# A streaming encoder step: the query projection as a set of seven block products

## The chip, the cores and the metric

The kernel runs on one core of a Trainium2 chip. The metric is the device time of one execution in microseconds. Before the change it was 788.36 us, the median of 3 runs (787.86 to 789.13).

## The reference, cut to what matters

The reference is one layer of an encoder for 528 frames of a new stream (16 meta frames and 512 of the prompt) and 64 frames of a running one, with caches of 1024 keys and values.

```
hp = layer_norm(concat(meta, x_prompt), ln_in_g, ln_in_b)      # 528 x 1024
hs = layer_norm(x_sample, ln_in_g, ln_in_b)                    #  64 x 1024
z = h @ w_in + b_in
u, q, k, v, ga, gb = split(z, ...)        # u, q, k, v: 512 columns each; ga, gb: 1024 each
pooled  = trailing window means of u, minus u
attn    = stick_breaking_attention(q, k and v with the cache), 8 heads of 64
mix = sigmoid(ga) * (pool_out @ w_br_pool) + sigmoid(gb) * (attn @ w_br_attn)
h = layer_norm(ALPHA * h + mix @ w_out + b_out, ...)
h = layer_norm(ALPHA * h + square(relu(h @ w_mlp1 + b1)) @ w_mlp2 + b2, ...)
```

The queries `q` of the 512 prompt frames and the 64 sample frames (576 columns; the meta frames have no queries), scaled by 1/8, are the part that the change computes in another way.

## The kernel before, in words

Everything lies transposed: channels on the 128 partitions, frames along the row. Every product is computed in fp32r in three matmuls, high part by high part, high by low and low by high, so each weight and each operand is rounded into a high part by ScalarE (ACT) and the rest is subtracted into a low part by VectorE (DVE). Weights come as units of 128 x 1024: all eight chunks of the input for 128 output channels. SyncE (SP) loads them into four raw slots; `split` makes `whi` and `wlo` in two slots. A unit is 48 matmuls: 2 halves of the frames, 8 chunks, 3 parts.

*The first normalisation* works on `r0`, 8 chunks of channels by 592 frames in two halves of 296. For the second half VectorE scales a chunk (`scale0`, L2258), ScalarE adds the bias and rounds it to `h_hi` (L1481), and VectorE makes `h_lo` (L2264), chunk 0 to chunk 7. The counter `n0_scaled` is 16 when the last chunk is scaled.

*The keys* (`keys_pair`, L877 to L880) are four units. Units 0 and 1 run together for a half of the frames, in the two banks of `lin`, the second some chunks behind the first; then units 2 and 3. The second half of units 0 and 1 follows the normalisation chunk by chunk. `key_out(m, h)` on ScalarE (L1494) moves the bank to `k_t` and frees it: `key_out(0, 1)` frees the bank of unit 2's second half and `key_out(1, 1)` that of unit 3's.

*The queries* are four more units (`linear`, L757 to L759) from the 576 frames in two halves of 288; ScalarE and VectorE move them to `q_t` and `q_s` (by head, for the sample frames). Then come `scores(0)` (L978), the first scores of the sample frames against the cache, and the value units (L938 to L940). Before its first matmul `scores(0)` waits for the keys' cache, for the masks of GpSimd (POOL), and for `consts`, a counter that ScalarE raises behind the copies of two small triangular matrices, `tri_r` (L1541) and `below_r` (L1542). `weighted_values(0)` is the first to want the values' cache.

*Sets.* Most of the MLP runs in twelve sets of seven block products after the scheme of Strassen and Winograd: the weights of four output units and the operand are cut in two by two blocks, seven products of sums of blocks take the place of eight. The seven weight operands (`W_AL` to `W_GA`) come from five loaded blocks, two of them with a second block added by an accumulating load that GpSimd issues, and from two additions on VectorE (`x_sum`, `dp_sum`); `op_hi` (L1859) and `op_lo` (L2717) split them. `block_product` (L1274 to L1276) issues the 24 matmuls of one product (2 output banks, 4 chunks, 3 parts). A product waits for its low part (`s_lo`), its moving operand and its banks; ScalarE copies two results (`first_copy`, `second_copy`) and VectorE adds two (`third_sum`, `fourth_sum`). The moving sums (`hs_sum`: V5, V6, T3, V4, each of four chunks by 288 frames) are made once for all sets (L2812, L2816, L1928).

The order of each engine's work is the order of its program, written out by hand; engines meet only at counting semaphores.

## Time and profile before

| | us |
|---|---|
| median of 3 runs | 788.36 |
| lowest, highest | 787.86, 789.13 |
| the profiled execution's own time | 788.11 |
| its span, first to last instruction | 786.4 |
| TensorE busy | 773.2 (98%) |
| VectorE busy | 521.4 (66%) |
| ScalarE busy | 427.4 (54%) |
| GpSimd busy | 145.7 (19%) |
| granted clock, mean | 0.995 |

The profile is of one execution, and its terms are counted against its own 788.11 us. PE stands for TensorE's matmuls and PEld for its weight loads, which lie beside them. Matmuls are pipelined: a record of some 0.3 us starts every 0.13 us, so the pitch is read from the starts and not from the durations.

### The profile page before, as it was taken

How to read it: one execution, taken by the hardware profiler on the slowest of the kernel's cores; microseconds unless marked ns; L12 is line 12 of the kernel's file. 1: busy time of each engine (PE TensorE's matmuls, PEld its weight loads, DVE VectorE, ACT ScalarE, POOL GpSimd, SP SyncE). 2: the span in 40 equal slices, each digit the busy share in tenths (PEclk: the TensorE clock that was granted, in tenths of full speed). 3: DMA queues.
4: the chain of work that ended last, by engine and by line, in shares of the span. 5: the costliest groups of instructions: out<-in, count | busy, mean ns of one | idle time of the engine just before them, and what ended most of it. 6: DMA issues, size and time to landing. Idle time of an engine off the chain costs nothing.

```text
span 786.4 us, 14056 instructions
## 1 busy us (share of the span) xinstructions
PE 773.2 (98%) x5720; PEld 746.3 (95%) x5720; DVE 521.4 (66%) x762; ACT 427.4 (54%) x666; POOL 145.7 (19%) x195
## 2 busy tenths in 40 slices
PE   8999999999999999999999999999999999999995
PEld 6999889999989899999999999999999999999994
DVE  5833334756546466887769897778876897665744
ACT  4632445656556465564446566488436773477324
POOL 2100000390321110005560000000000000000456
PEclk9999999999999999999999999999999999999998
DMA  8732231111120212225111556655767566633203
GB/s 293 289 119 81 80 117 54 54 55 59 54 81 30 79 37 72 82 93 176 55 55 30 132 159 163 180 131 173 188 161 188 150 165 168 162 106 135 81 2 120
DMA packets 27070, 90.57 MB, mean 115 GB/s; under 512 B 2864, under 2 KB 7104, under 8 KB 26624
## 3 DMA queue, kind: packets, MB, share of 16 engines
q1 hardware_dynamic: 22592, 74.26, 27.5%
q0 software_dynamic: 4000, 15.10, 10.7%
q8 instruction: 45, 0.74, 0.4%
q10 hardware_dynamic: 416, 0.33, 0.1%
q14 instruction: 17, 0.14, 0.1%
HBM read 84.84 MB, written 4.85 MB: 114 GB/s over the span
## 4 chain that ended last, share of the span: by engine, by line
PE 93%; DVE 2%; ACT 2%; issue 1%; DMA 1%; SPq 0%; DVEq 0%; ACTq 0%
PE lin L757 9%; PE z L1274 8%; PE z L1275 8%; PE z L1276 8%; PE lin L758 8%; PE lin L759 8%; PE z L1013 3%; PE lin L1274 3%; PE lin L1275 3%; PE lin L1276 3%; PE lin L1151 3%; PE lin L1152 3%; PE lin L1153 3%; PE lin L1290 2%; PE lin L1289 2%; PE lin L1288 2%
## 5 line engine op out<-in xcount | busy, mean ns | idle before, releaser
L757 PE MATMUL lin<-h_hi,whi 128*128 128x288 f32 (+1 forms) x448 | 133.8, 299 | 0.0
L758 PE MATMUL lin<-h_lo,whi 128*128 128x288 f32 (+1 forms) x448 | 132.5, 296 | 0.0
L759 PE MATMUL lin<-h_hi,wlo 128*128 128x288 f32 (+1 forms) x448 | 132.0, 295 | 0.0
L757 PEld LDWEIGHTS lin<-h_hi,whi 128*128 128x128 f32 x448 | 84.2, 188 | 1.3 <-issue 1.1
L758 PEld LDWEIGHTS lin<-h_lo,whi 128*128 128x128 f32 x448 | 84.2, 188 | 0.1
L759 PEld LDWEIGHTS lin<-h_hi,wlo 128*128 128x128 f32 x448 | 84.3, 188 | 0.0
L2717 DVE TENSOR_TENSOR wlo<-raw,whi 128x1024 fp32r<-128x1024 f32 x48 | 58.7, 1224 | 20.8 <-ACT whi L1859 20.8
L1859 ACT ACTIVATE whi<-raw 128x1024 fp32r<-128x1024 f32 x48 | 50.7, 1056 | 37.1 <-PE z L1276 24.5
L2120 DVE TENSOR_TENSOR wlo<-raw,whi 128x1024 fp32r<-128x1024 f32 x41 | 50.9, 1241 | 28.6 <-ACT whi L1381 26.6
L1381 ACT ACTIVATE whi<-raw 128x1024 fp32r<-128x1024 f32 x38 | 40.0, 1053 | 50.6 <-PE lin L759 32.6
L1274 PE MATMUL z<-f_ops,whi 128*128 128x288 f32 x176 | 52.2, 296 | 0.2
L1275 PE MATMUL z<-f_ops,whi 128*128 128x288 f32 x176 | 51.6, 293 | 0.0
L1276 PE MATMUL z<-f_ops,wlo 128*128 128x288 f32 x176 | 51.4, 292 | 0.0
L3236 POOL DMA_DIRECT2D raw<-w_sets x12 | 10.4, 870 | 152.6 <-DMA raw<-w_sets 152.6
L2717 DVE TENSOR_TENSOR third_lo<-raw,third_hi 128x1024 fp32r<-128x1024 f32 x24 | 29.4, 1223 | 11.7 <-ACT third_hi L1859 11.5
L1859 ACT ACTIVATE third_hi<-raw 128x1024 fp32r<-128x1024 f32 x24 | 25.3, 1056 | 21.4 <-PE z L1276 10.1
L2341 DVE SCALAR_TENSOR_TENSOR sa<-z,sa 128x512 f32<-128x512 f32 (+4 forms) x25 | 19.8, 795 | 25.6 <-ACT sa L1564 25.4
L1274 PEld LDWEIGHTS z<-f_ops,whi 128*128 128x128 f32 x176 | 33.0, 188 | 0.6 <-issue 0.6
L1276 PEld LDWEIGHTS z<-f_ops,wlo 128*128 128x128 f32 x176 | 33.1, 188 | 0.0
L1275 PEld LDWEIGHTS z<-f_ops,whi 128*128 128x128 f32 x176 | 33.0, 188 | 0.0
L2304 DVE TENSOR_SCALAR gates<-lin,vecs 128x288 f32<-128x288 f32 x16 | 8.2, 515 | 34.7 <-PE lin L759 34.7
L3238 POOL DMA_DIRECT2D raw<-w_sets x12 | 10.4, 863 | 106.7 <-DMA raw<-w_sets 106.7
(456 smaller groups left out, 2590.7 us busy)
## 6 DMA issues: line engine op xcount, KB each, us to landing
raw<-w_stream SPq DMA_DIRECT2D x64, 512.0 KB, 3.3
raw<-w_sets SPq DMA_DIRECT2D x48, 512.0 KB, 3.9
raw<-w_sets POOLq DMA_DIRECT2D x24, 512.0 KB, 5.6
w_fifth<-w_sets SPq DMA_DIRECT2D x12, 512.0 KB, 7.0
r<-x_t SPq DMA_DIRECT2D x8, 296.0 KB, 5.1
kcache<-k_cache SPq DMA_DIRECT2D x1, 2048.0 KB, 10.2
vcache<-v_cache SPq DMA_DIRECT2D x1, 2048.0 KB, 8.9
y<-r SPq DMA_DIRECT2D x8, 160.0 KB, 1.8
```

The costliest lines, as they stand in the source:

```text
L757: pe.matmul(out, w_h, hi, start=first, stop=False)
L758: pe.matmul(out, w_h, lo, start=False, stop=False)
L759: return pe.matmul(out, w_l, hi, start=False, stop=last)
L1013: last = pe.matmul(zf[:, d:d + w], stationary[:, :], part[:, src + at:src + at + w], start=False, stop=True, skip_group_check=True)
L1151: pe.matmul(out, w_h, hi, start=first, stop=False)
L1274: pe.matmul(out, w_h, hi, start=s < 2 and i == 0, stop=False, skip_group_check=True)
L1275: pe.matmul(out, w_h, lo, start=False, stop=False, skip_group_check=True)
L1276: last = pe.matmul(out, w_l, hi, start=False, stop=i == PRS - 1, skip_group_check=True)
L1381: nc.scalar.activation(whi[:, j % SPLIT, :], raw[:, j, :], ACT.Copy).then_inc(hi_split, 1)
L1859: nc.scalar.activation(op_home(o)[0], set_home(source_slot(s)), ACT.Copy).then_inc(s_hi, 1)
L2120: tt(wlo[:, j % SPLIT, :], raw[:, j, :], whi[:, j % SPLIT, :].bitcast(F32), ALU.subtract)\
L2717: tt(home[1], set_home(source_slot(s)), home[0].bitcast(F32), ALU.subtract).then_inc(s_lo, 1)
```

## The change

The four query units go from the stream of weights and become one more set, the first of thirteen (`FIRST = 1` is the first of the old ones; the counters get offsets). Its output blocks go through `query_block` to `q_t` and `q_s`. Its moving sums come from `r0`: V5, V6 and V4 on VectorE, T3 with one subtraction and four small instructions on GpSimd, and `xs_round` and `xs_low` split them. Its first and every third weight operand, its fifth block and two results have rooms of their own in the memory of the values' cache and the normalisation, so the values' cache is loaded behind the whole set, as are the pool's state and the units behind them. Three of the eight warm matmuls at the start write to another bank.

```diff
 # constants
-SETS = [("out", 0, 0), ("out", 0, 1)]
+SETS = [("query", 0, 0), ("out", 0, 0), ("out", 0, 1)]
+FIRST = 1
...
 # SyncE, behind the loads of units 0 to 3
-            load_unit(1, 0)
-            load_unit(1, 1)
+            for n, slot, block, landed in ((1, c, 2, si_base), (2, a, 0, al_in), (3, d, 2, ap_base), (4, b, 1, de_in),
+                                           (4, g, 3, ga_in)):
+                sp.wait_ge(lo_split, n)
+                load_block(0, slot, block, landed)
             sp.dma_start(bv[:, :], bv_d).then_inc(bv_in, 16)
             sp.dma_start(kcache[:, :, :], kc_d).then_inc(kc_in, 16)
-            load_unit(1, 2)
-            load_unit(1, 3)
+            sp.wait_ge(s_lo, W_SI + 1)
+            sp.wait_ge(x_made, 1)
+            load_unit(1, 0, first=True)
...
+            sp.wait_ge(s_lo, W_GA + 1)
+            sp.wait_ge(op_done, OPS)
             sp.dma_start(vcache[:, :, :], vc_d).then_inc(vc_in, 16)
             sp.dma_start(wpool[:, :, :], wpool_d).then_inc(wpool_in, 16)
...
 # TensorE, behind the keys
-            for m in range(4):
-                linear(1, m, N_Q + m, h_hi, h_lo, META, HA)
...
+            for s in range(OPS):
+                block_product(0, s)
...
 # ScalarE
             for k in range(4, KC):
                 norm0_hi(k, 1)
+            op_hi(0)
             key_out(0, 1)
-            act.wait_ge(unit_in[0], 32)
-            act.wait_ge(unit_done, 1)
-            nc.scalar.activation(whi[:, 0, :], raw[:, 0, :], ACT.Copy).then_inc(hi_split, 1)
-            for m in range(1, 4):
-                key_out(m, 1)
+            xs_round(V5)
+            op_hi(1)
+            key_out(1, 1)
+            key_out(2, 1)
+            xs_round(V6)
+            key_out(3, 1)
 
             act.wait_ge(bq8_done, 1)
-            for m in range(4):
-                split_next(1, m)
-                act.wait_ge(half_done, N_Q + m + 1)
-                nc.scalar.activation(q_t[:, m, 0:HA], lin[:, 0, 0:HA], ACT.Identity, bias=bq8[:, m:m + 1],
-                                     scale=SB_SCALE).then_inc(bank_free[0], 1)
+            act.wait_ge(q_zero, 1)
+            for s in range(OPS):
+                if s == 1:
+                    first_copy(0)
+                    xs_round(T3)
+                elif s == 2:
+                    second_copy(0)
+                elif s == 3:
+                    xs_round(V4)
+                elif s == 6:
+                    query_block(C12)
+                if s + 2 < OPS:
+                    op_hi(s + 2)
+                if s in (4, 5):
+                    query_block(C11 if s == 4 else C22)
+                if s == 5:
+                    act.wait_ge(op_done, 5)
+                    split(1, 0)
+            act.wait_ge(op_done, 6)
+            split(1, 1)
+            query_block(C21)
 
             act.wait_ge(made, 7)
             nc.scalar.activation(tri_r[:, :], tri[:, :], ACT.Copy)
...
 # VectorE, behind the low part of chunk 7 and a product of 4 columns
+            xs_sum(V5)
+            op_lo(0)
+            x_sum(0)
+            xs_sum(V6)
+            xs_low(V5)
+            op_lo(1)
+            xs_sum(V4)
+            xs_low(V6)
+            for s in range(OPS):
+                if s == 3:
+                    third_query()
+                elif s == 5:
+                    fourth_query()
+                if s + 2 < OPS:
+                    op_lo(s + 2)
+                if s == 1:
+                    dp_sum(0)
+                    xs_low(T3)
+                elif s == 3:
+                    xs_low(V4)
             split(1, 0)
...
 # GpSimd, in the middle of the masks
+            add_blocks(0)
...
+            pool.wait_ge(vecs_in, 16)
+            nc.gpsimd.tensor_tensor(xb_diff[:, :], vecs[:, V_LNIN_B + PRS:V_LNIN_B + KC],
+                                    vecs[:, V_LNIN_B:V_LNIN_B + PRS], ALU.subtract).then_inc(made, 1)
             pool.wait_ge(n0_scaled, 2 * KC)
-            pool.dma_start(u_t[:, :, UP:UP + STATE], state_d).then_inc(state_in, 16)
+            c = slice(META + HA, T)
+            nc.gpsimd.tensor_tensor(xs_sums[:, T3 - V5, :, :], r0[:, PRS:KC, c], r0[:, 0:PRS, c], ALU.subtract)\
+                .then_inc(made, 1)
+            pool.wait_ge(made, 13)
+            for k in range(PRS):
+                x_k = xs_sums[:, T3 - V5, k, :]
+                nc.gpsimd.tensor_scalar(x_k, x_k, 1.0, xb_diff[:, k:k + 1], ALU.mult, ALU.add).then_inc(made, 1)
```

## Rows read from the trace of the kernel before

**Rows 1.** The page: TensorE's busy time; the granted clock in 40 slices.
```profile
PE 773.2 (98%) x5720; PEld 746.3 (95%) x5720; DVE 521.4 (66%) x762; ACT 427.4 (54%) x666; POOL 145.7 (19%) x195
PEclk9999999999999999999999999999999999999998
```
**Rows 2.** Waits of PE: us in total, times, longest.
```profile
PE lin L877 <- ACT h_hi L1481: 0.8, 1, 0.8
```
**Rows 3.** Timeline of PE (start us, us): first query matmul, first behind the queries.
```profile
49.63 0.30 PE L757 MATMUL lin<-h_hi,whi 128*128 128x288 f32 x1
...
75.12 0.38 PE L978 MATMUL z<-q_s,k_t 128*128 128x128 f32 x2
```
**Rows 4.** Lines of the block products (ns min/median/max, first and last start).
```profile
L1274 PE MATMUL z<-f_ops,third_hi x80: 291/294/371, 454.6 to 677.1; 128*128 128x288 f32 x80
...
L1276 PE MATMUL z<-hs_hi,wlo x96: 293/295/298, 506.0 to 722.0; 128*128 128x288 f32 x96
```
**Rows 5.** Timeline of VectorE, at the end of the normalisation.
```profile
40.21 0.52 DVE L2264 SCALAR_TENSOR_TENSOR h_lo<-r,vecs,h_hi 128x296 fp32r<-128x296 f32 x1
40.91 0.53 DVE L2264 SCALAR_TENSOR_TENSOR h_lo<-r,vecs,h_hi 128x296 fp32r<-128x296 f32 x1 [0.17 <-ACT h_hi L1481]
41.35 0.20 DVE L2300 TENSOR_SCALAR bq<-vecs 128x4 f32<-128x4 f32 x1
```
**Rows 6.** GpSimd's groups by form (busy us, mean ns, idle before).
```profile
L3105 POOL TENSOR_SCALAR win<-win 128x591 f32<-128x591 f32 x4 | 3.5, 876 | 0.4
...
L3243 POOL TENSOR_TENSOR sum<-r 128x576 f32<-128x576 f32 x1 | 1.4, 1430 | 47.5 <-DVE r L2934 47.5
```
**Rows 7.** Timelines of GpSimd and VectorE, where they meet.
```profile
391.73 0.80 POOL L3211 TENSOR_TENSOR sumsq<-sumsq,sq 128x288 f32<-128x288 f32 x1
...
391.81 1.03 DVE L2571 SCALAR_TENSOR_TENSOR h_lo<-r,vecs,h_hi 128x288 fp32r<-128x288 f32 x1
...
158.27 1.80 POOL L3111 TENSOR_TENSOR u_t<-win,u_t 128x591 f32<-128x591 f32 x1
...
159.34 1.81 DVE L2120 TENSOR_TENSOR wlo<-raw,whi 128x1024 fp32r<-128x1024 f32 x1 [0.15 <-ACT whi L1381]
```
**Rows 8.** Timeline of PE in the keys: last of unit 0, first of unit 3.
```profile
41.71 0.30 PE L880 MATMUL lin<-h_lo,whi 128*128 128x296 f32 x1
...
45.12 0.29 PE L877 MATMUL lin<-h_hi,k_hi 128*128 128x296 f32 x1
```
**Rows 9.** Lines of the sets' sums, roundings and splits (ns min/median/max).
```profile
L2812 DVE TENSOR_TENSOR hs_sums<-r x1: 1351/1351/1351, 437.1 to 437.1; 128x1152 f32<-128x1152 f32 x1
...
L1928 ACT ACTIVATE hs_hi<-hs_sums x4: 1146/1150/1157, 478.6 to 491.1; 128x1152 fp32r<-128x1152 f32 x4
...
L2816 DVE SCALAR_TENSOR_TENSOR hs_sums<-hs_sums,vecs,r x4: 512/512/514, 460.8 to 462.1; 128x288 f32<-128x288 f32 x4
...
L2717 DVE TENSOR_TENSOR wlo<-raw,whi x48: 1217/1224/1228, 453.1 to 710.7; 128x1024 fp32r<-128x1024 f32 x48
...
L1859 ACT ACTIVATE whi<-raw x48: 1042/1060/1064, 449.8 to 709.7; 128x1024 fp32r<-128x1024 f32 x48
```
**Rows 10.** Timeline of ScalarE at the end of the queries.
```profile
72.14 0.50 ACT L1537 ACTIVATE q_t<-lin,bq 128x288 f32<-128x288 f32 x1 [2.07 <-PE lin L759]
...
72.74 0.30 ACT L1542 ACTIVATE below_r<-below 128x128 fp32r<-128x128 f32 x1
```
**Rows 11.** Loads: the page's issues (us to landing); timelines of SP and GpSimd.
```profile
raw<-w_sets POOLq DMA_DIRECT2D x24, 512.0 KB, 5.6
...
14.11 2.78 SPq L663 DMA_DIRECT2D raw<-w_stream  x2
...
40.61 0.97 POOL L3079 DMA_DIRECT2D u_t<-pool_state  x1 [5.55 <-DVE r L2258]
```
**Rows 12.** Timeline of PE at its end; a window (busy, PEclk, DMA, GB/s).
```profile
776.15 0.61 PE L1338 MATMUL z<-sq,inv 128*128 128x256 f32 x2
...
779.00:779.50 0.50, 0.00 (x0) 0.00 (x0) 0.47 (x2) 0.06 (x1) 0.50 (x2) 0.53 0.00 0
```

More of the change, by code:

```diff
@@ L847, in _ @@
             pe.wait_ge(made, 1)
-            for _ in range(WARM):
-                warm()
+            for n in range(WARM):
+                if n < 3:
+                    pe.matmul(z[:, 2, bass.ts(n, P)], inv_d[:, :], inv_d[:, :], start=n == 0, stop=True,
+                              skip_group_check=True)
+                else:
+                    warm()
             for p in range(KC // 2):
@@ new lines, in block_product @@
+            def block_product(t, s):
+                kind, p, g = SETS[t]
+                o, f = OPS * t + s, MOVING[ORDER[s]]
+                home, (chain, copy, second, third) = op_home(o), bank_pairs(t)
+                pair = (chain, second, chain, copy, chain, second if kind == "out" else third, chain)[s]
+                pe.wait_ge(s_lo, o + 1)
+                banks_ready(t, s)
+                moving_ready(t, s)
+                for j in range(2):
+                    out = one_bank(pair, j)
+                    if t < FIRST and s == 0:
+                        pe.wait_ge(bank_free[j], N_K + 4)
+                    for i in range(PRS):
+                        if t == FIRST and j == 0 and i in (0, PRS - 1):
+                            ready = max(F_AT[f, n] for n in (range(PRS - 1) if i == 0 else (i,)))
+                            pe.wait_ge(f_lo_done, ready + 1)
+                        at = slice((2 * i + j) * P, (2 * i + j + 1) * P)
+                        w_h, w_l = home[0][:, at], home[1][:, at]
+                        hi, lo = (f_op(f, i, 0), f_op(f, i, 1)) if kind == "out" else hs_op(f, i, t)
+                        pe.matmul(out, w_h, hi, start=s < 2 and i == 0, stop=False, skip_group_check=True)
+                        pe.matmul(out, w_h, lo, start=False, stop=False, skip_group_check=True)
+                        last = pe.matmul(out, w_l, hi, start=False, stop=i == PRS - 1, skip_group_check=True)
+                last.then_inc(op_done, 1)
@@ L1279, in _ @@
-            for t in range(N_SETS):
+            for t in range(FIRST, N_SETS):
                 for s in range(OPS):
@@ new lines, in query_block @@
+            def query_block(c):
+                chain, copy, _, third = bank_pairs(0)
+                if c == C22:
+                    act.wait_ge(z_summed, 2)
+                else:
+                    act.wait_ge(op_done, {C11: 4, C12: 6, C21: 7}[c])
+                scale = -SB_SCALE if c in (C22, C21) else SB_SCALE
+                for j in range(2):
+                    m = 2 * j + int(c in (C22, C21))
+                    src = q_fourth[:, j, :] if c == C22 else one_bank({C11: copy, C12: third, C21: chain}[c], j)
+                    if c in (C11, C21):
+                        last = nc.scalar.activation(q_t[:, m, 0:HA], src, ACT.Identity, bias=bq8[:, m:m + 1], scale=scale)
+                    else:
+                        nc.scalar.activation(q_t[:, m, HA:SEQ], src[:, 0:SEQ - HA], ACT.Identity, bias=bq8[:, m:m + 1],
+                                             scale=scale)
+                        for e in range(2):
+                            rows = slice(64 * e, 64 * e + 64)
+                            last = nc.scalar.activation(q_s[rows, 2 * m + e, :], src[rows, SEQ - HA:HA], ACT.Identity,
+                                                        bias=bq8[rows, m:m + 1], scale=scale)
+                    last.then_inc(relu_done, 1)
@@ new lines, in xs_sum @@
+            def xs_sum(o):
+                x = xs_sums[:, o - V5, :, :]
+                first, second = slice(META, META + HA), slice(META + HA, T)
+                if o == V5:
+                    tt(x, r0[:, 0:PRS, first], r0[:, 0:PRS, second], ALU.subtract).then_inc(hs_made, 1)
+                elif o == V4:
+                    dve.wait_ge(hs_made, 1 + PRS)
+                    for k in range(PRS):
+                        stt(out=x[:, k, :], in0=xs_sums[:, V6 - V5, k, :], scalar=vec(V_LNIN_B + PRS + k),
+                            in1=r0[:, PRS + k, first], op0=ALU.subtract, op1=ALU.subtract).then_inc(hs_made, 1)
+                else:
+                    dve.wait_ge(hs_made, 1)
+                    for k in range(PRS):
+                        stt(out=x[:, k, :], in0=xs_sums[:, 0, k, :], scalar=vec(V_LNIN_B + PRS + k),
+                            in1=r0[:, PRS + k, second], op0=ALU.add, op1=ALU.add).then_inc(hs_made, 1)
```

356 lines of the change are left out of this document (194 added, 162 removed).

## Prediction

> **What bounds the kernel now.** I read the page first: TensorE (PE) is busy in 773.2 of 786.4 us, and its granted clock is full in every slice but the last [rows 1]. Then the waits of PE: behind the first microseconds the longest in the whole span is one of 0.8 us [rows 2], for the first normed frame; the others are smaller still. So what PE issues, one matmul after the other, is the time, and an edit is worth what it takes from PE's list or adds to its waits. The stage of the change is the queries. Its first matmul starts at 49.63 us and the first of the stage behind it at 75.12 [rows 3]: 25.49 us for 192 matmuls, 132.8 ns each. The block products that the kernel has already run at the same pitch: from 454.6 to 722.0 us it issues 2016 matmuls [rows 4], 132.7 ns each, with no wait of weight in all twelve sets.
>
> **Fewer matmuls.** Four units of 48 are 192. One set has seven products of 2 x 4 x 3, which are 168. The 24 that go are worth 24 x 132.8 ns = 3.19 us. This is all that the change can bring.
>
> **What must be ready for the set, and where it is put.** Every step that follows goes by the three other engines in the last 10 us of the keys, where the new work is queued.
>
> *The third moving sum on GpSimd.* It waits for all 16 normed frames. The last scaling is the instruction in front of the low part at 40.21 us in VectorE's list (its `n0_scaled` comes near 40.3) [rows 5]. The sum is a subtraction of 1152 elements with both inputs in SBUF. GpSimd's 576-element one takes 1430 ns and its 288-element ones 0.80 us [rows 6, 7]: 2.2 ns an element and 0.16 us, so 2.7 us here. The trace shows what such an instruction does to a VectorE one with two SBUF inputs that starts beside it. At 391.81 us a 288-element low part takes 1.03 us in place of 0.52 (as at 40.21), with a GpSimd addition running from 391.73 to 392.53; at 159.34 a 1024-element one takes 1.81 in place of 1.22, with one running to 160.07 [rows 5, 7]. In both VectorE ends as if it had begun 0.1 to 0.2 us before GpSimd's record ended (392.84 - 0.52 = 392.32; 161.15 - 1.22 = 159.93): it waits for the whole GpSimd instruction. In the new kernel VectorE holds the way until 40.73 (the low part of chunk 6), then is idle till 40.91, as it waits for ScalarE [rows 5]. GpSimd starts there, at about 40.6, and ends at 43.3. The low part of chunk 7, at 40.91 now, is then done at about 43.6 in place of 41.44. It is the operand of PE's matmul at 41.71 [rows 8]. PE waits until 43.65: **1.95 us**, with everything behind it. From both sides: nothing, if VectorE's instruction gets in first or both share the way; 2.2 us, if GpSimd's is not held up at its start. I take the value of the two rows, which agree.
>
> The Trainium skill, page "SBUF — State Buffer", section "SBUF: two separate sides", states this as a lock: the pair of ports that VectorE and GpSimd share is held for the whole instruction by the one that starts first, and counts for a VectorE instruction with two SBUF inputs against a GpSimd one that reads SBUF. By that rule this term is about 2 us, and the trace agrees with its 1.03 and 1.81 us; were the ports a shared bandwidth instead, the term would be under 0.7 us.
>
> *The first rounding ahead of the second key output.* `xs_round(V5)` and `op_hi(1)` stand in ScalarE's list ahead of `key_out(1, 1)`, which frees the bank that PE wants for the first matmul of unit 3 at 45.12 [rows 8]. `xs_round` needs the sum V5 of VectorE: 1.35 us [rows 9], behind the low part and the tiny product at 41.35 [rows 5]. With the 1.95 us above: low part until 43.6, tiny product, then the wait for one of GpSimd's four small sums (591 elements take 0.88 us in the mean [rows 6], so some 0.5 us each) until 43.9, the sum until 45.2, the rounding (1.15 [rows 9]) until 46.4, `op_hi(1)` (1.06 [rows 9]) until 47.35, `key_out` (as long as the output at 72.14, 0.50 [rows 10]) until 47.8. PE wants the bank at 45.12 + 1.95 = 47.07. **0.76 us** of wait. Without the GpSimd term the same sum reads 42.83, 44.0, 45.0, 45.4 against 45.12: 0.4 us with the restart. With two small GpSimd sums in the way it is 1.2. The keys end 2.7 us late, at 52.34.
>
> *The set.* Product s starts at 52.34 + 3.19 s. VectorE's list up to the low part of the third operand is the first sum, two sums of four pieces (4 x 0.43 each), two low parts of 1.35, three low parts of weights and one sum of weights (1.22 each) [rows 9], 12.4 us at full durations and 11.4 back to back. With some 0.4 us for each of GpSimd's small sums it is done at 56.7, and product 2 wants it at 58.7: hidden, with 2.0 us to spare. From there each weight operand is released by a product two steps back, as in the sets of before, and the copies, the third and fourth sum (0.8 us) fit between; the tightest is the third sum, with about 1.1 us to spare. The blocks come long before: SP issues the first at 14.1 us where it issues unit 4 now, the accumulating load takes 5.6 us to land, and it is wanted at 46 [rows 11]. The two loads that GpSimd issues wait for blocks in its list, ahead of the masks; these are wanted by PE at 75 us, and GpSimd is idle for the 5.6 us before 40.61 [rows 11]. The values' cache is issued behind product 6, and SP's loads of units behind it; the cache is wanted behind the scores and all four value units, the next unit of weights (raw slot 0, the first of the pooling branch) behind three of them. Each costs nothing; if one of these covers were gone its lateness counts in full.
>
> *From the set to the scores.* This is the wait that the text of the diff hides. `scores(0)` waits for `consts`, which ScalarE raises behind two small copies, and these stand behind `query_block(C21)`, which waits for the **last** product. Now they end at 73.04 (the second is at 72.74), behind the output of the half that PE finished 3.2 us before its end [rows 3, 10]. After the change: 0.20 us from PE's end to ScalarE, two outputs at a pitch of 0.40 and the first copy at 0.20 (together the 0.60 from 72.14 to 72.74), 0.30 for the second, and 0.05 to PE: 0.2 + 0.8 + 0.2 + 0.3 + 0.05 = **1.55 us** in which PE has nothing. At its lower end 1.3 (a quicker release), at its upper one 2.0 (`split(1, 1)`, put ahead of it, ends 0.6 us before and may be late). The warm matmuls that change their bank, and the counters that are renumbered, cost nothing: the count is the same.
>
> **The sum.** Against the profiled execution's own 788.11 us: 788.11 - 3.19 + 1.95 + 0.76 + 1.55 = 789.18. Behind the scores PE alone sets the order, so the shift is kept to the end. That execution lies 0.25 us below the median of 788.36, so I forecast **789.4**. A difference of 0.2% (1.6 us) is about what a measurement of this kernel can tell from none.
>
> **The rivals.**
> *A: the GpSimd sum does not stop the low part.* The sum is then 788.11 - 3.19 + 0.4 + 1.55 = 786.9, on the median's scale 787.1. For it: GpSimd's start after its release isn't shown for this place (its load at 40.61 now starts 0.3 us after the release [rows 11]), and many pairs in the trace run side by side with no loss. Against it: both rows of a pair with two SBUF inputs.
> *B: the waits are hidden and the whole 3.2 us is seen*, 785.2. It wants both the bank and `consts` early; the list of ScalarE speaks against it.
> *C, slower: VectorE falls behind and product 2 waits.* Its list of 11.4 us and GpSimd's small sums have 2.0 us to spare in front of product 2. If each of those sums (0.9 us each at worst) stops it in full, or the four-piece sums are stopped by each other, it is 2 us later yet; from the point where 2.0 us are used up each further us is one of PE. With 1.5 us over: 790.9. A late accumulated block would have the same face.
> *D, slower: the clock.* PE's last matmuls start at 776.15, and the granted clock, still 1.00 at 779.0, falls towards 0.50 (1.2 GHz; 0.53 in the mean to 779.5) [rows 12], over 2 us after they end. The longest wait that I forecast is 1.95 us, just short of that; the one of 0.8 us left the clock at full [rows 1, 2]. If it falls, every us at the lower level costs half: with 2 to 4 us of it 790.4 to 791.4.
>
> **How the numbers follow.** Forecast 0.58, its own range 788.7 to 790.4; A 0.17; B 0.06; C 0.13; D 0.06. The range from 786.6 to 791.4 takes in A and most of C and D and leaves out B and the far ends of C. Faster by over 0.2% (below 786.8): B, a third of A, and a little of the rest, 0.15. Slower by over 0.2% (above 789.9): C, D and a fifth of the forecast, 0.30. Within: 0.55.
>
> **What would show it.** In the profile after: the low part of chunk 7 (`h_lo`) as long as 2.7 us at 40.9, with GpSimd's 1152-element subtraction beside it, and PE idle before its `h_lo` matmul at 43.6; PE idle again for about 0.8 us before a key matmul near 47, released by ScalarE's `k_t`; 168 matmuls of the set in 22.3 us; and PE idle for about 1.5 us before the first matmul with `q_s`, released by `below_r`. If the low part takes 0.53 us, A is right. If PE waits inside the set for VectorE, C is. If PE's granted clock has a dip near 43 us, D is. The forecast is wrong if the first matmul with `q_s` comes before 75.6 us or behind 76.9.

## The result and the profile after

The changed kernel takes **792.41 us** (median of 5 runs, 791.38 to 793.42) where the kernel before takes 787.86 beside it: ratio 1.0055, interval 1.0044 to 1.0066. In a second comparison (`a1_after`) it was 791.66 against 788.01, ratio 1.0046, 1.0032 to 1.0061. So it is slower by 3.6 to 4.3 us by the ratios. Forecast were 789.4 and at most 791.4. Wherever this document says how much an edit brings, it compares ratios to the kernel before, taken beside each run, and 0.001 is 0.79 us; the interval of a ratio is some 1 us to either side. Two executions of the runs below were slow ones and are left out of every figure: 2673.15 us in `a1_after` (with it that run's median would be 792.11, a number that some of the expectations use) and 838.29 us in `e2_bank_first`, which is the profiled one, so that its profile is not read.

The profiled execution of the changed kernel takes 791.38 us, with a span of 789.6. Its page begins:

```profile
PE 771.1 (98%) x5695; PEld 743.8 (94%) x5696; DVE 537.7 (68%) x770; ACT 440.2 (56%) x687; POOL 156.1 (20%) x203
...
PEclk9999999999999999999999999999999999999998
```

TensorE has 2.1 us less to do [rows 1] and the span is 3.2 us longer, so it waits more. The waits of PE in the whole span (us in total, times, longest):

```profile
PE z L1079 <- ACT below_r L1672: 2.3, 1, 2.3
PE lin L922 <- DVE h_lo L2364: 1.9, 2, 1.7
PE z L897 <- DVE pair L2309: 1.2, 2, 0.6
...
PE lin L919 <- issue: 0.5, 1, 0.5
```

The first, the second and the last of these are new beside [rows 2]. The one between them (`pair`) stands at the head of the kernel, in a part that the change leaves as it was: VectorE adds pieces of x in pairs, each as soon as its load has landed. VectorE starts the fourth of these sums between 6.8 and 8.5 us in the profiles of this case, in the kernel before at 7.32, here at 8.14; this is called the head below. The timeline of PE around the new waits (start us, us; in brackets the idle time before and its releaser):

```profile
42.45 0.29 PE L920 MATMUL lin<-h_hi,wlo 128*128 128x296 f32 x1
44.49 0.40 PE L922 MATMUL lin<-h_lo,whi 128*128 128x296 f32 x1 [1.75 <-DVE h_lo L2364]
...
47.85 0.30 PE L922 MATMUL lin<-h_lo,k_hi 128*128 128x296 f32 x1
48.66 0.37 PE L919 MATMUL lin<-h_hi,k_hi 128*128 128x296 f32 x1 [0.51 <-issue]
...
53.24 0.29 PE L1017 MATMUL lin<-h_hi,q_third_hi 128*128 128x288 f32 x1
...
75.40 0.30 PE L1019 MATMUL lin<-xs_hi,q_third_lo 128*128 128x288 f32 x1
77.98 0.46 PE L1079 MATMUL z<-q_s,k_t 128*128 128x128 f32 x2 [2.28 <-ACT below_r L1672]
```

The set runs from 53.24 to 75.53 (the last start and one pitch of 0.13): 22.29 us for 168 matmuls, and none of them waits. What released the wait for the low part stands in the timeline of VectorE,

```profile
41.77 2.66 DVE L2364 SCALAR_TENSOR_TENSOR h_lo<-r,vecs,h_hi 128x296 fp32r<-128x296 f32 x1 [0.17 <-ACT h_hi L1533]
```

and in that of GpSimd beside it:

```profile
41.24 2.87 POOL L3241 TENSOR_TENSOR xs_sums<-r 128x1152 f32<-128x1152 f32 x1 [5.18 <-DVE r L2358]
44.22 5.35 POOL L3246 TENSOR_SCALAR xs_sums<-xs_sums,xb_diff 128x288 f32<-128x288 f32 x4
```

The low part takes 2.66 us where it took 0.53 [rows 5]; GpSimd's record of the subtraction ends at 44.11, and VectorE's low part ends at 44.43 as if it had begun at 43.9. What released the two others, the bank and the constants, stands in the timeline of ScalarE:

```profile
48.07 0.49 ACT L1546 ACTIVATE k_t<-lin,vecs 128x296 f32<-128x296 f32 x1
...
74.68 0.62 ACT L1605 ACTIVATE q_s<-z,bq 64x64 f32<-64x64 f32 x2
75.32 1.06 ACT L1433 ACTIVATE whi<-raw 128x1024 fp32r<-128x1024 f32 x1
76.41 0.89 ACT L1599 ACTIVATE q_t<-lin,bq 128x288 f32<-128x288 f32 x2
77.19 0.31 ACT L1671 ACTIVATE tri_r<-tri 128x128 fp32r<-128x128 f32 x1
77.39 0.31 ACT L1672 ACTIVATE below_r<-below 128x128 fp32r<-128x128 f32 x1
```

The output that frees the bank ends at 48.56, PE starts at 48.66. The first matmul with `q_s` starts 2.86 us later than before [rows 3]. By starts of PE, this is the account: head +0.82, low part +1.96 (1.75 of idle time and the restart), bank +0.67 (48.66, where 47.99 would follow at the pitch), set -3.20 (22.29 for 25.49), constants +2.45 (77.98 against 75.53), and 0.16 in small pieces. The head varies from execution to execution with the landing. Without it, the profile says that the change costs some **1.9 us**. The ratios say 3.6 to 4.3. So two things are to be found: what each wait is made of, and where about 2 us more come from that this profile doesn't have.

### The profile page after: what moved, and what is told of

Same layout as the page of the kernel before. It is cut to its first block, busy times and chain, and to the rows that moved or that the text cites. A ratio compares the mean times of both kernels' runs of the same rounds, so it can differ in the third digit from the quotient of the medians.

```text
span 789.6 us, 14042 instructions
## 1 busy us (share of the span) xinstructions
PE 771.1 (98%) x5695; PEld 743.8 (94%) x5696; DVE 537.7 (68%) x770; ACT 440.2 (56%) x687; POOL 156.1 (20%) x203
## 4 chain that ended last, share of the span: by engine, by line
PE 90%; ACT 3%; DVE 3%; issue 2%; DMA 1%; SPq 0%; DVEq 0%; ACTq 0%
PE z L1017 9%; PE z L1018 9%; PE z L1019 9%; PE lin L794 7%; PE lin L795 7%; PE lin L796 7%; PE lin L1017 3%; PE lin L1018 3%; PE lin L1019 3%; PE z L1114 3%; PE lin L1252 3%; PE lin L1253 3%; PE lin L1254 3%; PE lin L1342 2%; PE lin L1340 2%; PE lin L1341 2%
## 5 line engine op out<-in xcount | busy, mean ns | idle before, releaser
L794 PE MATMUL lin<-h_hi,whi 128*128 128x288 f32 (+1 forms) x384 | 114.9, 299 | 0.0
L795 PE MATMUL lin<-h_lo,whi 128*128 128x288 f32 (+1 forms) x384 | 113.6, 296 | 0.0
L796 PE MATMUL lin<-h_hi,wlo 128*128 128x288 f32 (+1 forms) x384 | 113.2, 295 | 0.0
L794 PEld LDWEIGHTS lin<-h_hi,whi 128*128 128x128 f32 x384 | 72.2, 188 | 1.3 <-issue 1.1
L795 PEld LDWEIGHTS lin<-h_lo,whi 128*128 128x128 f32 x384 | 72.2, 188 | 0.1
L796 PEld LDWEIGHTS lin<-h_hi,wlo 128*128 128x128 f32 x384 | 72.3, 188 | 0.0
L3209 POOL DMA_DIRECT2D raw<-w_sets x13 | 11.5, 882 | 153.3 <-DMA raw<-w_sets 153.3
L3211 POOL DMA_DIRECT2D raw<-w_sets x13 | 11.3, 866 | 116.3 <-DMA raw<-w_sets 116.3
```

What stands on the lines that cost most here:

```text
L794: pe.matmul(out, w_h, hi, start=first, stop=False)
L795: pe.matmul(out, w_h, lo, start=False, stop=False)
L796: return pe.matmul(out, w_l, hi, start=False, stop=last)
```

## The experiments

Theory at the start: three waits (GpSimd's subtraction, the bank, the constants), each to be had back by one move in a list. Rivals: the low part is late because the query units have moved, not because of GpSimd; VectorE's list is too long; and the granted clock of TensorE, which shows no dip in this profile.

**Each wait by itself.** `e1_sum_behind`, GpSimd waits for VectorE's first sum and so for the low part in front of it:

```diff
             pool.wait_ge(n0_scaled, 2 * KC)
+            pool.wait_ge(hs_made, 1)
             c = slice(META + HA, T)
```

> The changed kernel with one edit: GpSimd's subtraction of 1152 elements waits for VectorE's first moving sum as well. Theory of the shared way: the low part of chunk 7 takes 0.53 us in place of 2.66, TensorE's wait of 1.75 us for it is gone, 1.7 to 2.0 us less in all. If the low part were late for another reason (ScalarE's rounding, the frames), nothing changes. The wait for the bank of unit 3 may stay at 0.3 to 0.7 us.

Measured: 788.96, ratio 1.0013 (1.0004 to 1.0022), 1.0 us above the kernel before. The wait for the low part is gone, and only one new long one is left:

```profile
PE z L1079 <- ACT below_r L1672: 2.2, 1, 2.2
...
PE lin L1017 <- DVE wlo L2429: 0.3, 1, 0.3
```

This one edit brings 2.6 to 3.3 us. By the starts of its profile it should bring 1.5: the low part's 1.96 are gone and the bank's wait falls from 0.67 to 0.28, but 0.4 and 0.6 us come at two places in the set (product 0's second bank, and operand 2). So over a microsecond more comes back than was waited.

`e3_copies_first`, the copies of the constants ahead of ScalarE's part of the set:

```diff
             act.wait_ge(q_zero, 1)
+            act.wait_ge(made, 7)
+            nc.scalar.activation(tri_r[:, :], tri[:, :], ACT.Copy)
+            nc.scalar.activation(below_r[:, :], below[:, :], ACT.Copy).then_inc(consts, 1)
             for s in range(OPS):
...
             query_block(C21)
 
-            act.wait_ge(made, 7)
-            nc.scalar.activation(tri_r[:, :], tri[:, :], ACT.Copy)
-            nc.scalar.activation(below_r[:, :], below[:, :], ACT.Copy).then_inc(consts, 1)
```

> The changed kernel with one edit: the copies tri_r and below_r, which raise consts, ahead of the set and not behind its last output. Theory of the waits: TensorE's 2.3 us before the first matmul with q_s falls to 0.2 us or less, 2.1 to 2.5 us less in all. Rival: the scores then wait for the third output block (ScalarE ends it at 75.3 us, the set ends at 75.5) and half of the gain stays away. Theory of the clock: with this longest wait gone the executions that lie 1 to 2 us above the profiled one come down more than it does.

Measured: 788.54, ratio 1.0003 (0.9994 to 1.0012). PE has no wait at the scores; the one for the low part stays (2.0, of which 1.75 at 44.82). The edit brings 3.4 to 4.1 us, again more than its wait of 2.45 (and its own profile has half clock behind the low part, see below).

`e2_bank_first`, the output that frees unit 3's bank ahead of the rounding:

```diff
             key_out(0, 1)
+            key_out(1, 1)
             xs_round(V5)
             op_hi(1)
-            key_out(1, 1)
```

> The changed kernel with one edit: key_out(1, 1) ahead of xs_round(V5) and op_hi(1). Theory of the waits: the wait of 0.5 to 0.7 us before unit 3 is gone and nothing else moves, 0.6 us less. Rival: the bank was free anyway and the 0.5 us of issue is something else; no change.

Measured: 792.21, ratio 1.0052 (1.0039 to 1.0066), nothing that stands out from the changed kernel's 1.0055 and 1.0046. It was run once more, as `a2_bank_first`, to see where its 0.67 us go.

> The changed kernel with the output of unit 1's second bank ahead of the rounding and the high part, once more, since its gain was 0.1 to 0.2 us where 0.6 were expected. If the wait moves on, the profile shows no wait at the first matmul of unit 3 and 0.4 us or more at the second bank of product 0, released by the last key output, which stands behind V6's rounding. If it is the clock, unit 3 stands in a stretch at half clock in which the bank would have been free in time anyway, and the edit is worth nothing there.

Measured: 791.68, ratio 1.0039 (1.0025 to 1.0053). In its profile the wait of 0.5 is gone and nothing has taken its place between 43.3 and 75 us: the bank was the wait, and the first branch (it moves on) is wrong. The second is borne out by the profiles in which half clock comes behind the low part (below): the kernels `e3_copies_first` and `e7_split_last` have the changed kernel's order, and PE doesn't wait for the bank in them. In them ScalarE frees the bank at 48.88 and 48.58, and PE, at half clock, comes to it only after that. So the profiles say that the edit is worth 0.67 in some executions and nothing in others; by the medians its gain can't be told from nothing.

`e4_all_three`, the three edits together:

> The changed kernel with its three waits of TensorE taken away: GpSimd's third moving sum also waits for VectorE's first one (so it starts behind the low part of chunk 7), key_out(1, 1) stands ahead of xs_round(V5) and op_hi(1), and the two copies that raise consts stand ahead of the set. Theory of the waits: the profile loses 1.96 + 0.66 + 2.45 = 5.1 us against the changed kernel's 791.4, so some 786.3 us, about 1.6 us under the kernel before; the first matmul with q_s starts near 73 us. Theory of the set (the set itself, its loads or what follows costs the time): over 790 us. Theory of the clock (in the executions beside the profiled one the granted clock falls in the waits of 2 us): the spread of the changed kernel, 791.4 to 793.4, shrinks to under 1 us, and no execution has a mean clock under 0.995.

Measured: **786.41**, ratio 0.9977 (0.9968 to 0.9986): faster than the kernel before, by 1.8 us (1.6 were forecast) and not by 3.2. All of its mean clocks are 0.995 to 0.997. Two waits that the three had covered are left in it; PE's waits:

```profile
PE lin L1017 <- ACT k_t L1546: 0.5, 1, 0.5
PE lin L1017 <- DVE wlo L2429: 0.3, 1, 0.3
```

What makes them stands in the timeline of VectorE,

```profile
43.74 3.72 DVE L2415 TENSOR_TENSOR raw<-raw 128x1024 f32<-128x1024 f32 x1
47.38 2.78 DVE L2445 SCALAR_TENSOR_TENSOR xs_sums<-xs_sums,vecs,r 128x288 f32<-128x288 f32 x4
```

and in that of GpSimd:

```profile
42.83 3.55 POOL L3242 TENSOR_TENSOR xs_sums<-r 128x1152 f32<-128x1152 f32 x1 [7.72 <-DVE xs_sums L2436]
46.49 3.38 POOL L3247 TENSOR_SCALAR xs_sums<-xs_sums,xb_diff 128x288 f32<-128x288 f32 x4
```

The subtraction no longer stops the low part; it stops the sum of the blocks, the third large operation behind the low part (3.72 us for 1.22), and the four small operations stop V6's sum (2.78 for 1.80). The last key output stands behind V6's rounding, so the second bank of product 0 is late, and operand 2's low part too.

**GpSimd alone.** `m1_before_sum` adds only the subtraction to the kernel before (and lets the copies of the constants wait for the higher count that goes with it, which makes no wait of PE at the scores in its profile):

```diff
...
-            act.wait_ge(made, 7)
+            act.wait_ge(made, 12)
             nc.scalar.activation(tri_r[:, :], tri[:, :], ACT.Copy)
...
             pool.wait_ge(n0_scaled, 2 * KC)
+            c = slice(META + HA, T)
+            nc.gpsimd.tensor_tensor(spare[:, :, :], r0[:, PRS:KC, c], r0[:, 0:PRS, c], ALU.subtract).then_inc(made, 1)
```

> The kernel before with one thing added: GpSimd subtracts 1152 elements a lane of the normed frames from 1152 others, into room that nobody reads, as soon as the last piece is scaled. The rest, the four query units as units among it, stands as before. If the subtraction stops VectorE's low part of chunk 7 for its whole length, that part takes about 2.7 us where it took 0.5, the first matmul that reads it waits about 1.8 to 1.9 us, and the time is 1.8 to 2 us above the kernel before. If only the move of the query units made the wait, the low part keeps its 0.5 us and the time stays within 0.3. If a wait of 2 us at this place also lowers TensorE's granted clock in most executions, the time is 2.7 to 3.2 us above the kernel before, and the mean granted clocks of the executions lie at 0.992 to 0.994 where those of the kernel before lie at 0.995 to 0.997.

Measured: 791.10 against 788.01, ratio 1.0037 (1.0024 to 1.0050), 2.9 us; mean clocks 0.994 to 0.995. The timeline of VectorE:

```profile
41.20 2.66 DVE L2265 SCALAR_TENSOR_TENSOR h_lo<-r,vecs,h_hi 128x296 fp32r<-128x296 f32 x1 [0.18 <-ACT h_hi L1482]
```

That of PE:

```profile
43.92 0.52 PE L881 MATMUL lin<-h_lo,whi 128*128 128x296 f32 x1 [1.75 <-DVE h_lo L2265]
44.24 0.45 PE L878 MATMUL lin<-h_hi,whi 128*128 128x296 f32 x1
44.48 0.45 PE L879 MATMUL lin<-h_hi,wlo 128*128 128x296 f32 x1
...
47.20 0.42 PE L878 MATMUL lin<-h_hi,k_hi 128*128 128x296 f32 x1
47.44 0.32 PE L879 MATMUL lin<-h_hi,k_lo 128*128 128x296 f32 x1
47.60 0.30 PE L881 MATMUL lin<-h_lo,k_hi 128*128 128x296 f32 x1
```

The subtraction makes the whole wait, with no other part of the change in the kernel: that the moved query units make it is out. And here is what the first profile of the changed kernel didn't have. Behind the wait the matmuls go at a pitch of 0.25 us and not 0.136, and the windows of this profile (busy time of PE, PEld, DVE, ACT, POOL; granted clock, DMA share, GB/s) say why:

```profile
43.00:44.00 1.00, 0.08 (x1) 0.08 (x1) 0.94 (x2) 0.00 (x0) 1.00 (x2) 1.00 0.00 0
44.00:45.00 1.00, 1.00 (x5) 1.00 (x6) 0.00 (x0) 0.52 (x2) 0.46 (x1) 0.52 0.00 0
45.00:46.00 1.00, 1.00 (x6) 1.00 (x6) 0.04 (x1) 0.93 (x1) 0.00 (x0) 0.50 0.22 31
46.00:47.00 1.00, 1.00 (x6) 1.00 (x6) 1.00 (x1) 0.30 (x1) 0.00 (x0) 0.50 0.00 0
47.00:48.00 1.00, 1.00 (x7) 1.00 (x7) 0.19 (x1) 0.21 (x1) 0.00 (x0) 0.77 0.00 0
```

TensorE is granted the lower of its two levels, 1.2 GHz for 2.4, from just behind 44.0 to about 47.5 us, while it is busy again. 13 matmuls at 0.11 us more each are 1.4 us.

**The changed kernel again.** `a1_after`, no edit:

> The changed kernel as it is, on the chip of the runs beside it. The waits of its first profile should come back: 1.9 us for the low part of chunk 7, 0.8 for a bank of unit 3, 2.3 for the copied constants. If the microsecond by which its median lies above its profiled execution comes from TensorE's clock, executions with a mean granted clock of 0.992 to 0.994 take about 1 us more than those with 0.996, and a profile of such an execution shows a stretch below 1.00 behind one of the waits that the first profile has at full clock. If it comes from the loads' landing, the first chunks start later in it and the clocks are alike.

Measured: 791.66. The waits come back (2.2 for `below_r`, 2.0 for `h_lo`, 0.5 for the bank), and its profiled execution has a mean clock of 0.994; the windows of PE:

```profile
44.00:48.00 4.00, 3.51 (x26) 3.29 (x25) 4.00 (x5) 2.74 (x4) 4.00 (x3) 1.00 0.00 0
...
77.00:78.00 1.00, 1.00 (x6) 1.00 (x6) 0.00 (x0) 0.00 (x0) 0.00 (x0) 0.50 1.04 442
78.00:79.00 1.00, 1.00 (x7) 1.00 (x6) 0.00 (x0) 0.00 (x0) 0.00 (x0) 0.50 1.03 442
79.00:80.00 1.00, 1.00 (x7) 1.00 (x6) 0.00 (x0) 0.00 (x0) 0.00 (x0) 0.50 1.05 420
```

This time the fall comes behind the wait for the constants (PE starts again at 76.72) and not behind the low part. Over ten executions of the changed kernel: two with a mean clock of 0.996 at 790.0 and 791.4; four with 0.994 at 791.7 to 793.1; four with 0.992 at 792.3 to 793.4. Each step of 0.002 is one stretch of 3.4 us at half clock (3.4 x 0.5 / 790 = 0.002). The mean alone is a blunt sign, though: behind the last matmuls of every profile the clock stands at half for another 5 to 8 us, as in [rows 12], and that alone makes it 0.995 to 0.997. So 0.995 can hide one stretch (`e3_copies_first`, profiled with one) or none (`e6_round_later`); 0.994 and 0.992 go with one and two in the profiles.

**The constants' wait.** `e7_split_last` was to test that ScalarE's list makes it:

```diff
-            split(1, 1)
             query_block(C21)
+            split(1, 1)
             act.wait_ge(made, 7)
```

> The changed kernel with one edit: ScalarE's second split of the values' weights (1.06 us) goes behind the last query block's two outputs, so the outputs and the copies of the constants begin at the end of the set and not 0.85 us later. If the wait before the first matmul with q_s is ScalarE's queue (split, outputs, copies), it falls from 2.3 us to 1.2 to 1.5, and the time by 0.8 to 1.1. If that wait is set by something that doesn't stand in this queue, it stays at 2.3. What could take the gain back: the values' first product needs the split, and would then wait at its start by up to 0.3 us.

Measured: 792.73, ratio 1.0059 (1.0047 to 1.0071), and a wait of 2.6, not 1.2 to 1.5. (One of its six executions, 794.70, has a mean clock of 0.945; without it the median is 792.24.) A miss, and the edit's own fault: the split stands behind the outputs, but still ahead of the copies, and these are what raises `consts`. The list adds up to it all the same: outputs 0.10 us behind PE's end at 76.53, 0.78 for them, 0.94 for the split, 0.50 for the two copies, 0.26 to PE at 79.11. In its profile both waits are followed by half clock (0.50 from 45 to 48 and from 80 to 82 us), at a mean of 0.992.

`e8_split_behind` puts the split behind the copies too.

> The changed kernel with ScalarE's second split of the values' weights behind the last query block's outputs and behind the copies of the constants too, so that from the set's end only outputs (0.89) and copies (0.5) stand ahead of the first matmul with q_s. If the 2.3 us there are ScalarE's list and nothing else, the wait falls to 1.3 to 1.6. The time then falls by 0.8 to 1.0 where the clock stands as it did, and by 1.5 to 2.3 (to 790 to 791) if the shorter wait also leaves the clock at full speed behind it, which the mean clocks would show (0.994 and above where the changed kernel has 0.992 to 0.994). If the wait is set by something else it stays at 2.3.

Measured: 790.64, ratio 1.0029 (1.0018 to 1.0040), 1.3 to 2.1 us under the changed kernel. The timeline of ScalarE:

```profile
74.56 0.89 ACT L1599 ACTIVATE q_t<-lin,bq 128x288 f32<-128x288 f32 x2 [0.53 <-PE lin L1019]
75.34 0.31 ACT L1670 ACTIVATE tri_r<-tri 128x128 fp32r<-128x128 f32 x1
75.54 0.31 ACT L1671 ACTIVATE below_r<-below 128x128 fp32r<-128x128 f32 x1
```

The timeline of PE:

```profile
76.10 0.46 PE L1079 MATMUL z<-q_s,k_t 128*128 128x128 f32 x2 [1.64 <-ACT below_r L1671]
```

With the split out of the way the wait is 1.64, against the forecast's 1.55. So the sum was right for the list that it wrote down, and the split was what it lacked. Seven of eight executions have mean clocks of 0.995 to 0.997, though the wait for the low part is in this kernel as before.

**The clock by itself.** Two runs fill the waits and leave every other engine as it is. `m2_sum_filled` is `m1_before_sum` with 12 more matmuls in the wait; `f2_after_filled` is the changed kernel with these and 15 more in the wait for the constants:

```diff
+                if (m, h, k) == (0, 1, KC - 1):
+                    for _ in range(12):
+                        pe.matmul(z[:, 3, 0:HT], h_hi[:, k, 0:P], h_hi[:, k, c], start=True, stop=True)
                 pe.wait_ge(n0_lo, KC * h + k + 1)
...
+                    pe.wait_ge(relu_done, 6)
+                    for _ in range(15):
+                        pe.matmul(z[:, 3, 0:HT], h_hi[:, 0, 0:P], h_hi[:, 0, 0:HT], start=True, stop=True)
                     pe.wait_ge(consts, 1)
```

> The kernel before with GpSimd's extra subtraction, and TensorE fills the wait for the low part of chunk 7: 12 more matmuls of 296 columns (12 x 0.137 = 1.6 us) into a bank that is free there and that nobody reads. The low part is as late as without them. If half clock behind the wait is what makes the measured price 3.1 us where the wait is 1.8, the executions lie at 1.8 to 2.1 us above the kernel before, their mean clocks at 0.995 to 0.997, and the profile shows 1.00 from 42 to 50 us. If the price has another cause (the lock lasts longer in most executions, or what comes behind the unit is late), the filling changes nothing: 2.7 to 3.2 us above, at the clocks of the kernel without it.

Measured: 790.78, ratio 1.0026 (1.0014 to 1.0037), 2.1 us above the kernel before where the unfilled one is 2.9 (2.5 and 3.1 by the medians); all clocks 0.996 or 0.997. The two intervals overlap, so this pair alone doesn't prove the gain; the clocks do differ.

> The changed kernel with both of its long waits filled: 12 more matmuls of 296 columns ahead of the low part of chunk 7, and 15 (2.0 us) behind the wait for the third query block's outputs, ahead of the wait for the copied constants; all into a bank that is free there and that nobody reads. Nothing else moves. If half clock behind these waits is what lifts the median of the changed kernel (792.1 to 792.4) above its executions at full clock (790.0 to 791.4), the median comes down to 790.2 to 791.0 and the mean clocks to 0.995 to 0.997. If the clock has no part in it, the median stays at 792 or goes above it, since the fillers can only end late.

Measured: **790.07** (11 runs, 789.26 to 790.76), ratio 1.0020 (1.0011 to 1.0029), with mean clocks of 0.995 to 0.997 in all of them. The timeline of PE in its profile:

```profile
42.32 1.79 PE L923 MATMUL z<-h_hi 128*128 128x296 f32 x12
44.26 0.40 PE L925 MATMUL lin<-h_lo,whi 128*128 128x296 f32 x1 [0.15 <-DVE h_lo L2370]
...
75.31 2.20 PE L1074 MATMUL z<-h_hi 128*128 128x296 f32 x15
77.49 0.49 PE L1085 MATMUL z<-q_s,k_t 128*128 128x128 f32 x2
```

And of VectorE:

```profile
41.51 2.70 DVE L2370 SCALAR_TENSOR_TENSOR h_lo<-r,vecs,h_hi 128x296 fp32r<-128x296 f32 x1 [0.17 <-ACT h_hi L1539]
```

The low part is as late as it was, TensorE does 3.7 us of useless work, and the kernel is 2.0 to 2.8 us faster for it by the ratios (790.07 for 792.37, the median of the ten executions above, is 2.3), with intervals that don't overlap. 1.6 to 1.75 us are left above the kernel before: the account of the waits at full clock (1.96 + 0.67 + 2.45 - 3.20 = 1.88). The spread goes as well, from 3.4 us between the fastest and the slowest to 1.5. This is the experiment that shows the clock as the cause: nothing else was changed, and what PE waits for comes no earlier. (The two kernels were each measured beside the kernel before and not side by side; `a2_bank_first`, on the same chip as `f2_after_filled`, has 1.0039 and four of five mean clocks at 0.994.)

**Does anything stand against the whole 3.2 us?** `e5_vector_sum` is `e4_all_three` with the moving sum T3 taken from GpSimd and made by VectorE behind operand 2:

```diff
...
+                elif o == T3:
+                    dve.wait_ge(made, 12)
+                    for k in range(PRS):
+                        stt(out=x[:, k, :], in0=r0[:, PRS + k, second], scalar=xb_diff[:, k:k + 1],
+                            in1=r0[:, k, second], op0=ALU.add, op1=ALU.subtract).then_inc(made, 1)
...
```

> The version with all three edits (subtraction later, bank's output first, copies of the constants first), and T3's moving sum taken from GpSimd altogether: VectorE makes it in four operations of 288 elements behind its low part of operand 2. GpSimd and VectorE then work on nothing at the same time there. If GpSimd's 7 us were what made VectorE late (its sum of the set's weights took 3.7 us for 1.1, V6's sum 2.8 for 1.8), both go back, the waits of 0.5 us for product 0's second bank and of 0.3 for operand 2 shrink to 0.2 or less together, and the time is 0.7 to 1.1 us under the version with three edits, 2.6 to 3.1 under the kernel before. If VectorE's own list is what is too long, T3's 1.8 us there make operand 3 or T3's rounding late, and the time stays at 786.0 to 786.8.

Measured: 786.05, ratio 0.9973 (0.9963 to 0.9983). Both stopped sums are back at 1.22 and 1.80 us and both waits are gone, but the time is where the rival has it. One wait is new, in the timeline of PE:

```profile
62.60 0.37 PE L1017 MATMUL lin<-xs_hi,whi 128*128 128x288 f32 x1 [0.60 <-issue]
```

The timeline of ScalarE shows its cause:

```profile
54.91 1.17 ACT L1584 ACTIVATE xs_hi<-xs_sums 128x1152 fp32r<-128x1152 f32 x1 [1.78 <-DVE xs_sums L2440]
55.99 1.04 ACT L1566 ACTIVATE q_third_hi<-raw 128x1024 fp32r<-128x1024 f32 x1
```

ScalarE waits for the new sum with operand 3's high part queued behind; VectorE then waits 2.18 us for that, and all that follows in its list is late. Product 4, due at 61.84, wants a bank that VectorE's third sum frees, and in this profile that sum runs from 61.74 to 62.50 (operand 4 itself was ready at 61.83). `e6_round_later` changes the order of these two:

```diff
                     first_copy(0)
-                    xs_round(T3)
...
                 if s + 2 < OPS:
                     op_hi(s + 2)
+                if s == 1:
+                    xs_round(T3)
```

> The version with T3's sum on VectorE, and ScalarE rounds that sum behind the high part of operand 3 and not ahead of it. In the version before it ScalarE waited 1.8 us at the rounding for VectorE's sum, with operand 3's high part behind it, which made VectorE 2.2 us late with the low parts, and product 4's matmul waited 0.6 us at 62.60. If that order made the wait, it goes (0.1 or less is left) and the time is 0.5 to 0.6 us lower, 785.4 to 785.6, 2.4 to 2.7 under the kernel before. If VectorE's 1.8 us more make the lists late in any order, a wait of 0.3 or more stands at another of the seven products and the time stays at 785.8 to 786.2.

Measured: **785.25** against 788.40, ratio 0.9956 (0.9942 to 0.9970). In its profile PE has no gap of over 0.1 us from 20 us on past the scores, and the first matmul with `q_s` starts at 72.73, 2.39 us before the one of [rows 3], in an execution whose head is 0.76 us later (its fourth pair starts at 8.08): 3.15. It is the fastest version, and it reaches the forecast's "all that the change can bring", 3.19 us. The expectation, 785.4 to 785.6, was missed by 0.15 us on the good side.

## Why the prediction was wrong

Against the kernel before, the prediction's sum is +1.07 us (789.18 for 788.11), and +3.6 to +4.3 were measured. The difference, 2.5 to 3.3 us, is made of two steps: the constants, 0.7 to 0.9, and the clock, 2.0 to 2.8.

*Fewer matmuls, -3.19:* right. 22.29 us for the set, -3.20; and in measured time -3.5 (-4.6 to -2.4) where nothing is in its way.

*GpSimd's subtraction, +1.95:* right, 1.96 in the profile, 2.1 (1.1 to 2.9) by the run that adds it alone with the wait filled. The length forecast for the low part was 2.7 and it took 2.66. Rival A is out. The page "SBUF — State Buffer" of the Trainium skill, section "SBUF: two separate sides", has the pair of ports locked for the whole instruction by whoever starts first; the trace agrees (2.66 us for 0.53), and the version with three edits shows the same lock at the next instruction when the first one is spared (3.72 for 1.22).

*The bank, +0.76:* right at full clock (0.67), and nothing where half clock comes ahead of it.

*VectorE's list, rival C:* it didn't happen in the changed kernel: operand 2 is ready 2.0 us before product 2, as forecast. But the late keys were what gave it room. With the first waits mended it shows, as idle times of 0.3 us for operand 2 and 0.5 for the last key output.

*The constants, +1.55:* mis-sized; measured 2.28 as idle time, 2.45 by starts. The step that failed is "0.20 us from PE's end to ScalarE". The prediction saw `split(1, 1)` ahead of the last block's outputs and let it end 0.6 us before the set does; it ended at 76.38, 0.68 us behind PE's last matmul (75.70). The queue in front of it was not added up: two blocks write `q_s` in pieces of 64 x 64, four each at 0.31 to 0.37 us; the first of them can't begin until VectorE's fourth sum (0.76 us, until 70.13) is done, and from 70.16 ScalarE has no gap up to the copies: a block, the first split, a block, the last split, the outputs. So the outputs start 0.71 us behind PE's end where 0.20 was taken, which is 0.5 of the 0.73; the other 0.23 are between `below_r`'s end and PE's start (0.28 where 0.05 was taken).

*The clock, rival D:* this is the larger part of the miss, 2.0 to 2.8 us. In the sum it stands at nothing. As a rival the prediction gave it 0.06 and priced it at 1 to 2 us on top of the forecast (2 to 4 us of half clock; each fall brought 3.4, and four executions of ten had two by their mean clocks), on the ground that the clock at the kernel's end falls over 2 us behind the last matmul [rows 12] and the longest wait would be 1.95. Both halves failed. The wait of 1.75 us was followed by half clock in three of the seven profiles read here that have it; what the clock does with nothing behind it, at the end of the kernel, did not say which waits are safe. And the long waits were not one but two, the second being 2.3 and followed by half clock in three of five profiles. With the terms as measured the sum without the clock reads 789.4 + 0.7 to 0.9 (constants) - 0.1 (bank), 790.0 to 790.2, and `f2_after_filled` has 790.07. The rest up to 791.66 and 792.41 is the clock.

The test at the end of the prediction, the first `q_s` matmul between 75.6 and 76.9, failed at 77.98, or 77.16 without the late head.

**What stays open.** Why the fall comes behind a given wait in one execution and not in the next. It was behind neither in the first profile of the changed kernel, behind the second in `a1_after` and `a2_bank_first`, behind both in `e7_split_last`. `e8_split_behind` keeps the first wait and has a second of 1.64, and only one of its eight executions has a mean clock under 0.995, where eight of the changed kernel's ten have: so what one wait does to the clock may hang on the other, and no run tests that. And the parts don't add up to the whole: the waits taken one at a time leave 0.5 to 0.8 us of clock behind each (0.8 between `m1_before_sum` and `m2_sum_filled`; `e1_sum_behind` is 1.0 us above the kernel before where the starts in its profile, at full clock and without the head, say 0.5; `e3_copies_first` 0.2 where the terms, -3.20 + 1.96 + 0.67, say -0.6), and together they cost 2.0 to 2.8. For `e1_sum_behind` the executions explain it: the eight at 0.996 and 0.997 have a median 0.6 us above the kernel before, and the other three, at 0.994 and 0.995, are 1.8 to 3.0 above. For `e3_copies_first` part of it is the bank: a stretch behind the low part costs 1.4 us and saves the bank's 0.67. The intervals, about 1 us each, allow for the rest; no run was made to settle it.

## What to carry to other kernels

A wait of TensorE costs its length and what the clock does behind it, here 1.4 us on top of a wait of 1.75 in the executions that had the fall; look for that in several executions, since the one that was profiled may be the one without the fall. When an operation moves to another engine, add up that engine's whole list to the moment where the critical wait ends, with every small piece in it; and what raises a semaphore that others wait for belongs ahead of work that nobody waits for. Spare one instruction a lock and look which one is next: here the gain came in full only when GpSimd had no large operation left beside VectorE's, and ScalarE's list was put in the order in which its inputs come.

## What the runs showed that was not expected

Half clock doesn't come during the wait, it comes behind it: in `m1_before_sum` the first matmul behind 1.75 us of nothing starts at 43.92 with the clock at 1.00 and the stretch at 0.50 begins just behind 44.0 and lasts 3.4 us, though TensorE is busy throughout. It is the same in all six such stretches of the profiles: each begins 0.0 to 1.4 us behind the restart of PE (1.35 in `a2_bank_first`, 0.01 behind the second wait of `e7_split_last`) and lasts 3.4 us. In the changed kernel's order such a stretch also swallows the wait of 0.67 us for the bank that follows it.

GpSimd's four operations of 288 elements in place, with one scalar a lane, took 5.35 us in the changed kernel and 3.38 in the version with three edits; one by one 0.59, 2.65, 1.46 and 0.70 there, and 1.35 and three times 0.69 here. In the changed kernel VectorE ran its sum V5, a low part, the sum of the blocks and part of V6's sum beside them, in the other only V6's sum and the end of the sum of the blocks. The subtraction took 2.87 and 3.55. So GpSimd is held up too, and not VectorE alone.
